# Rows of the last two expert items added by 0/1 products on TensorE, pair rows of the other items loaded during the expert loops

## The chip, the cores and the metric

The kernel is one program on one core of a Trainium2 chip. Its metric is the device time of one execution in microseconds (us), lower is better. Three executions of the kernel before took 1325.0, 1329.38 and 1330.95 us; the median is 1329.38 us.

## The reference, cut to what matters

Two layers of a backbone run over 256 context tokens and 256 latent tokens of 1024 numbers. A layer norms its tokens, projects them, mixes them in three head groups (SSD, long convolution, mLSTM), projects back and adds; then a second norm feeds a mixture of experts, whose output is multiplied by a gate vector and added to the stream. Of this the change touches the last part:

```
grp_prob = softmax(t @ grp_router_w + b);  group = argmax            # 4 groups
top_w, top_idx = top-2 of 8 experts inside that group                # 2 of 32 experts for each token
hid = silu(t @ w_gate[e]) * (t @ w_up[e])                            # 1024 -> 256
out[t] = sum over the token's two experts of top_w * (hid @ w_down[e])   # 256 -> 1024
x = x + mod[5] * out
```

In the first layer 512 tokens are routed (1024 token-expert pairs), in the last one only the 256 latent tokens (512 pairs). After the last layer the latent rows are normed once more and written out.

## The kernel before, in words

**Items.** The experts' work is cut into items: one expert with up to 64 of its tokens (`ITEM_ROWS`). Layer 0 has 33 items (`EXPERTS + EXTRA[0]`), layer 1 has 32. Three weight matrices of 1 MB belong to an item: gate, up, down. For item j GpSimd gathers the token rows from `h2_rows` in DRAM (`rows(j)`), TensorE transposes them (`gathered`), multiplies them by the gate and up matrices (`gate_up`), transposes the hidden rows (`hidden`) and multiplies by the down matrix (`down`). The result, scaled by the routing weight, goes to `res_v[:, j % 2, :]`: by ScalarE in layer 0 (`weighted`), by VectorE, with the gate vector too, in layer 1 (`gated_halves`). Its partitions 0 to 63 hold the first 512 numbers of the 64 rows, partitions 64 to 127 the other 512. GpSimd scatters it to `pair_rows` in DRAM: each token has two rows there, one for each of its experts (`y` = 0, 1).

**Weights.** SyncE (the queue SP) issues all weight loads in one order. Up to 18 places of SBUF (`pieces`) hold an expert matrix; `expert_slots` says which place the n-th matrix takes and behind the use of which earlier matrix (`behind`) it may be loaded. `taken_again` says whether a place is used again.

**The end of a layer.** After the last weight load SP issues the first two loads of the next layer's in-projection (`next(loading[l + 1])`, layer 0 only). Then it waits until the last two scatters have landed and loads `pair_rows`, one 1 MB DMA per token tile t of 128 tokens, in the order 2, 3, 0, 1 (layer 1: 2, 3) into the areas `two_v[l][t]` (L616, L618). All engines but SP and GpSimd meet at `stage_end(l, "moe")`. A block `If(flag != 0)` handles more than 33 (32) items; it isn't entered in the profiled execution.

**The start of layer 1.** VectorE works through the tiles: `pair_sum` (the two rows of a pair added), `pair_gate` (times the gate row), `pair_add` (added to `x`). ScalarE takes the squares of the new `x` for the norm. VectorE turns them into factors (`inverse`), the rows are scaled (`xn`, tile 2 by ScalarE, the others by VectorE), TensorE transposes them (L780) into all eight PSUM banks (`blocks`), ScalarE and VectorE copy them to `hT` (`input_columns`), and then the in-projection begins with the long convolution's columns (`hy`), which need the latent tiles 2 and 3 only. The context tiles 0 and 1 follow: their transposes (L761) stand on TensorE behind the first `hy` chunk and one product for the modulation, and wait for the rows `xn` of tile 1. `busy(b, n)` issues n products of no use, each two passes of 256 columns, while TensorE would else be idle: 11 ahead of the transposes of tile 2, 5 ahead of those of tile 3.

**The end of layer 1.** VectorE: sum 2, add 2, sum 3, `inverse(2)`, add 3, `normed_output(2)`, `inverse(3)`, `normed_output(3)`; then the output DMAs.

A bank of PSUM is taken in turn by `product(name)`, which makes TensorE wait at once until the bank's old content has been read. An fp32 product appears in the profile as two passes (records). L647 is the helper `mm`, L1778 `tt`, L1781 `stt`, L1784 `copy`, L1774 `ts`, L1391 `fn` (ScalarE).

## Time and profile before

| | us |
|---|---|
| executions | 1325.0, 1329.38, 1330.95 |
| the profiled execution: its time | 1326.25 |
| its span in the profile | 1324.4 |
| TensorE matmuls busy | 1169.2 (88%) |
| VectorE, ScalarE, GpSimd busy | 605.8 (46%), 305.8 (23%), 133.2 (10%) |

```profile
PE   6799999999889989999777689998889899998882
DVE  5434996038963641432111266973393533332223
ACT  4202112265352202131111232131442100000001
PEclk8899999999899989999998899998999899998897
DMA  8743233337651679999999745441474879999982
```

Each digit is the busy share in one of 40 equal slices of the span (33 us), in tenths. The stretches with a DMA digit of 9 (about 490 to 745 us and 1070 to 1290 us) are the two expert loops, where the 99 and 96 weight matrices stream in. PEclk is the granted clock of TensorE in tenths of 2.4 GHz. The boundary between the layers lies at 745 to 785 us.

### The profile page before, as it was taken

How to read it: one execution, taken by the hardware profiler on the slowest of the kernel's cores; microseconds unless marked ns; L12 is line 12 of the kernel's file. 1: busy time of each engine (PE TensorE's matmuls, PEld its weight loads, DVE VectorE, ACT ScalarE, POOL GpSimd, SP SyncE). 2: the span in 40 equal slices, each digit the busy share in tenths (PEclk: the TensorE clock that was granted, in tenths of full speed). 3: DMA queues.
4: the chain of work that ended last, by engine and by line, in shares of the span. 5: the costliest groups of instructions: out<-in, count | busy, mean ns of one | idle time of the engine just before them, and what ended most of it. 6: DMA issues, size and time to landing. Idle time of an engine off the chain costs nothing. (4 is left out here: it accounts for less than half of the span.)

```text
span 1324.4 us, 19485 instructions
## 1 busy us (share of the span) xinstructions
PE 1169.2 (88%) x7596; PEld 769.5 (58%) x7596; DVE 605.8 (46%) x1233; ACT 305.8 (23%) x623; POOL 133.2 (10%) x144
## 2 busy tenths in 40 slices
PE   6799999999889989999777689998889899998882
PEld 3444547977679855555444466467768655545551
DVE  5434996038963641432111266973393533332223
ACT  4202112265352202131111232131442100000001
POOL 0000000000000012222121100000000112221220
PEclk8899999999899989999998899998999899998897
DMA  8743233337651679999999745441474879999982
GB/s 288 200 157 110 82 111 96 100 121 233 206 193 38 261 260 382 390 384 371 374 390 376 268 158 166 128 141 48 160 269 187 350 303 391 386 389 395 397 338 111
DMA packets 146421, 321.40 MB, mean 243 GB/s; under 512 B 28217, under 2 KB 111222, under 8 KB 121368
## 3 DMA queue, kind: packets, MB, share of 16 engines
q1 hardware_dynamic: 134840, 304.08, 63.5%
q0 software_dynamic: 11392, 15.79, 3.7%
q8 instruction: 63, 1.03, 0.3%
q14 instruction: 30, 0.25, 0.1%
q10 hardware_dynamic: 96, 0.26, 0.0%
HBM read 320.32 MB, written 21.23 MB: 258 GB/s over the span
## 5 line engine op out<-in xcount | busy, mean ns | idle before, releaser
L647 PE MATMUL bank<-hT,ring 128*128 128x512 f32 (+1 forms) x544 | 207.4, 539 | 1.8 <-DVE hT L1774 1.8
L647 PE MATMUL bank<-ring,hT 128*128 128x256 f32 (+1 forms) x928 | 181.9, 351 | 8.4 <-DVE chain L1784 3.9
L647 PEld LDWEIGHTS bank<-ring,hT 128*128 128x128 f32 x928 | 155.2, 195 | 28.0 <-issue 7.0
L647 PE MATMUL bank<-chain,qkT 128*64 128x256 f32 (+1 forms) x792 | 144.8, 386 | 19.7 <-DMA chain<-in_moe_w_up 5.5
L647 PEld LDWEIGHTS bank<-hT,ring 128*128 128x128 f32 x544 | 104.2, 194 | 98.6 <-issue 91.7
L1778 DVE TENSOR_TENSOR ktok<-ktok,bank 64x256 f32<-64x256 f32 x65 | 27.5, 423 | 281.1 <-ACT ktok L1391 217.4
L1391 ACT ACTIVATE ktok<-bank 64x256 f32<-64x256 f32 (+2 forms) x79 | 32.1, 406 | 350.6 <-PE bank L647 295.6
L647 PEld LDWEIGHTS bank<-chain,qkT 128*64 128x64 f32 (+1 forms) x792 | 86.7, 152 | 40.0 <-issue 20.4
L1324 POOL DMA_INDIRECT pair_rows<-hyT,ysum x65 | 65.7, 1011 | 385.0 <-ACT hyT L1391 197.7
L647 PE MATMUL bank<-ring,qkT 128*64 128x256 f32 x528 | 84.1, 393 | 10.1 <-DMA ring<-in_moe_w_up 5.7
L1391 ACT ACT_TABLE_LOAD x33 | 42.3, 1283 | 111.2 <-PE bank L647 68.0
L1319 POOL DMA_INDIRECT big<-h_rows,ysum x65 | 61.7, 950 | 47.2 <-DVE ysum L1778 28.0
L647 PEld LDWEIGHTS bank<-ring,qkT 128*64 128x64 f32 x528 | 51.8, 141 | 25.1 <-issue 8.3
L647 PE MATMUL bank<-big,qkT 128*64 128x256 f32 x256 | 60.3, 390 | 1.8 <-DMA chain<-in_moe_w_up 1.4
L1333 POOL DMA_DIRECT2D grow<-in_b_mod x4 | 2.3, 584 | 589.0 <-ACT grow L1391 589.0
L1204 PEld LDWEIGHTS bank<-ident,big 64*128 64x128 f32 x520 | 37.6, 140 | 36.6 <-issue 24.8
L647 PE MATMUL bank<-ident 128*128 128x256 f32 x188 | 50.9, 426 | 8.7 <-DMA hT<-pair_rows 7.8
L647 PE MATMUL bank<-hT,qkT 128*64 128x256 f32 x272 | 50.6, 426 | 8.6 <-DMA hT<-in_moe_w_up 6.7
L1784 DVE COPY qkT<-bank 128x512 f32<-128x512 f32 x65 | 45.0, 692 | 24.1 <-PE bank L1204 22.3
L1204 PE MATMUL bank<-ident,big 64*128 64x64 f32 x520 | 46.1, 229 | 9.0 <-DMA big<-h_rows,ysum 5.3
L1227 PEld LDWEIGHTS bank<-ident,ktok 64*128 64x128 f32 x130 | 20.4, 204 | 55.0 <-DVE qkT L1784 37.3
L1778 DVE TENSOR_TENSOR big<-big,bank 128x384 f32<-128x384 f32 x48 | 26.6, 554 | 54.6 <-ACT big L1391 52.1
(298 smaller groups left out, 1718.0 us busy)
## 6 DMA issues: line engine op xcount, KB each, us to landing
ring<-in_w_mod SPq DMA_DIRECT2D x40, 1024.0 KB
chain<-in_moe_w_up SPq DMA_DIRECT2D x23, 1024.0 KB
ring<-in_w_in SPq DMA_DIRECT2D x22, 1024.0 KB
chain<-in_moe_w_down SPq DMA_DIRECT2D x19, 1024.0 KB
chain<-in_moe_w_gate SPq DMA_DIRECT2D x19, 1024.0 KB
ring<-in_moe_w_down SPq DMA_DIRECT2D x18, 1024.0 KB
ring<-in_moe_w_up SPq DMA_DIRECT2D x17, 1024.0 KB
ring<-in_moe_w_gate SPq DMA_DIRECT2D x16, 1024.0 KB
```

Source lines behind the costliest of these rows:

```text
L647: return nc.tensor.matmul(o, a, b, start=s, stop=e, **k)
L1204: last = nc.tensor.transpose(b[:, k * R:(k + 1) * R], rows_v[r0:r0 + R, j % 2, k * P:(k + 1) * P], ident[r0:r0 + R, r0:r0 + R])
L1227: last = nc.tensor.transpose(b[:, f * R:(f + 1) * R], hid_v[0:R, j % 2, f::2], ident[0:R, 0:R])
L1319: return nc.gpsimd.indirect_dma_start(dst, None, h2_rows, bass.IndirectOffsetOnAxis(at_, 0), bounds_check=NT * P - 1, oob_is_err=False)
L1324: return nc.gpsimd.indirect_dma_start(pair_halves, bass.IndirectOffsetOnAxis(at_, 0), src, None, bounds_check=2 * MOST_PAIRS - 1, oob_is_e ...
L1333: pool.dma_start(modrow(m)[2:3, :], A["b_mod"][l:l + 1, m * D:(m + 1) * D]).then_inc(gate_bias_in[l][n], tick(f"gate_bias{l}{n}_in", ("gat ...
L1391: step(nc.scalar.activation(o, i, f, **k), *names)
L1778: step(V.tensor_tensor(o, a, b, op), *names)
L1784: step(V.tensor_copy(o, a), *names)
```

## The change: what it does

- The results of a layer's last two items aren't scattered. From item `items_now - 6` on, VectorE has built 0/1 matrices (`late_rows`, `late_hot`): for each of the two items 64 rows by the 128 tokens of a tile, once for each half of the partitions. TensorE multiplies them with the results (`late`): four products for each tile, into two banks. VectorE adds the two banks to the summed pair rows (`pair_late`, two additions of 512 columns).
- Ahead of item 0's scatter, GpSimd scatters zeros to the rows of the last two items (`zeros scattered`), so that the sum over `pair_rows` is right without them.
- SP no longer waits for the last two scatters ahead of the pair loads, but for those of the two items before them. The areas of tiles 2 and 3 must be free by then: `PAIR_PLACES`, `LAST_IN_PAIRS` keep matrices with n > 82 out of them, so that later matrices take other places. The next layer's two first loads come behind the pair loads of tiles 2 and 3.
- TensorE and VectorE no longer wait for the other engines at the end of the expert stage; they do so inside `If(flag != 0)`.
- At the start of layer 1, VectorE's order becomes: sum 2, sum 3, late 2, gate 2, add 2, small columns, `inverse(2)`, late 3, gate 3, add 3, ... TensorE's becomes: `late` of tiles 2 and 3, small columns, transposes of tiles 2 and 3 with their `busy` products, `late` of tiles 0 and 1, in-projection. At the end of layer 1: sum, late, add of tile 2, then of tile 3, then `inverse(2)`.
- In layer 1 VectorE also clears `big[:, 0:2048]` during the out-projection (the gathered rows of an item beyond its tokens must be numbers now, since they are multiplied by 0).

The diff, cut to its core (left out: declarations, the constant `steps`, the block behind `flag`, where `res_more` takes the place of `res_v[:, 0, :]`):

```diff
+PAIR_PLACES, LAST_IN_PAIRS = ((4, 5), (14, 4)), 82
@@ -122,7 +123,7 @@
-    return l > 0 or s not in (8, 10) or n <= LAST_IN_TAPS
+    return (l > 0 or s not in (8, 10) or n <= LAST_IN_TAPS) and (s not in PAIR_PLACES[l] or n <= LAST_IN_PAIRS)
@@ -337,6 +340,11 @@
+        late_hot = (ktok[:, 0:1024].rearrange("p (n t c) -> p n t c", n=2, t=NT),
+                    ysum[:, 0:512].rearrange("p (n t c) -> p n t c", n=2, t=2))
+        late_token, late_step = ysum[:, 512:514], ysum[:, 514:530].rearrange("p (n b) -> p n b", n=2)
+        res_more = chain[:, 2048:2560]
@@ -494,7 +502,7 @@
                             for const, t in (("gsel", gsel), ("mask", ysum[:, 1024:1024 + 2 * P]), ("keep", keep),
-                                             ("iom", iom), ("inv", inv)):
+                                             ("iom", iom), ("inv", inv), ("steps", steps)):
@@ -594,10 +602,6 @@
-                if l + 1 < DEPTH:
...
-                    for _ in range(2):
-                        next(loading[l + 1])
@@ -612,10 +616,23 @@
-                for n in (1, 2):
+                def last_in(s):
+                    return ("used", ("expert", l, max(n for n in range(matrices) if places[n] == s)))
...
+                sp.wait_ge(*due(("zeros scattered", l)))
+                for n in (4, 3):
                     sp.wait_ge(*due(("scattered", l, EXPERTS + EXTRA[l] - n)))
-                for t, two in two_v[l].items():
-                    sp.dma_start(two, pair_rows.rearrange("(y t p) d -> t p y d", y=2, p=P)[t]).then_inc(
+                for t in two_v[l]:
+                    if t >= 2:
+                        sp.wait_ge(*due(last_in(PAIR_PLACES[l][t - 2])))
+                    elif t == 0:
+                        for _ in range(2):
+                            next(loading[l + 1])
+                        sp.wait_ge(*due(("made", ("gathered", l, EXPERTS + EXTRA[l] - 1))))
+                    else:
+                        sp.wait_ge(*due(last_in(8)))
+                        sp.wait_ge(*due(("made", ("spec", l + 1, 3))))
+                    sp.dma_start(two_v[l][t], pair_rows.rearrange("(y t p) d -> t p y d", y=2, p=P)[t]).then_inc(
@@ -722,6 +739,21 @@
+            def late(l, tiles):
...
+                items_now, t0 = EXPERTS + EXTRA[l], 0 if l == 0 else 2
+                b = {(t, half): product(("late", l, t, half)) for t in tiles for half in range(2)}
+                pe.wait_ge(*due(("late hot", l)))
+                for n in range(2):
+                    j = items_now - 2 + n
+                    pe.wait_ge(*due(("result", l, j)))
+                    for t in tiles:
+                        for half in range(2):
+                            rows = slice(ITEM_ROWS * half, ITEM_ROWS * half + ITEM_ROWS)
+                            last = mm(b[t, half][:, :], late_hot[l][rows, n, t - t0, :], res_v[rows, j % 2, :], n == 0, n == 1)
+                        if n:
+                            last.then_inc(pe_done, made(("late", l, t)))
@@ -769,17 +801,17 @@
                 else:
+                    late(l - 1, (2, 3))
...
                     for t in range(2):
-                        if t == 0:
-                            pe.wait_ge(*due(("pairs", l - 1, 2)))
...
                                 last.then_inc(pe_done, made(("h1", l, k, 1)))
+                    late(l - 1, (0, 1))
@@ -1259,8 +1291,10 @@
                 down(items_now - 1)
-                stage_end(l, "moe")
+                pe.drain().then_inc(pe_done, tick("pe_done", ("end", "pe", l, "moe")))
                 with pe.If(flag != 0):
+                    pe.wait_ge(*due(("end", "act", l, "moe")))
+                    pe.wait_ge(*due(("end", "dve", l, "moe")))
@@ -1292,6 +1326,8 @@
                     pe.wait_ge(more_dve[l], (MORE_ITEMS - EXTRA[l]) * MORE_DVE[l])
+                if l + 1 == DEPTH:
+                    late(l, (2, 3))
@@ -1355,9 +1391,15 @@
                         pool.wait_ge(*due(("pair table", l)))
+                        pool.wait_ge(*due(("zeros", l)))
+                        for late in (2, 1):
+                            scatter(res_v[:, 1, :], pair_of[:, items_now - late:items_now - late + 1]).then_inc(
+                                zeros_out[l], tick(f"zeros{l}_out", ("zeros scattered", l), by=16))
...
                         flag = pool.value_load(more_flag[0:1, :], min_val=0, max_val=MORE_ITEMS)
+                    if j >= items_now - 2:
+                        continue
@@ -1728,6 +1770,8 @@
                         act.wait_ge(*due(("scattered", l, j - 2)))
+                    elif j:
+                        act.wait_ge(*due(("zeros scattered", l)))
@@ -1814,6 +1858,13 @@
+            def pair_late(l, t):
+                two = two_v[l][t]
+                dve.wait_ge(*due(("made", ("late", l, t))))
+                for half in range(2):
+                    cs_ = slice(512 * half, 512 * half + 512)
+                    tt(two[:, 0, cs_], two[:, 0, cs_], bank(("late", l, t, half))[:, :], ADD, ("read", ("late", l, t, half)))
@@ -1894,10 +1945,7 @@
-                if l:
-                    step(V.memset(va_v[:, :, :, HD:HD + 1], 1.0))
-                    small_columns()
-                else:
+                if l == 0:
@@ -1931,12 +1979,16 @@
                     pair_sum(l - 1, 2)
-                    pair_gate(l - 1, 2)
-                    pair_add(l - 1, 2)
                     pair_sum(l - 1, 3)
-                    inverse(l, 2, 1)
-                    pair_gate(l - 1, 3)
-                    pair_add(l - 1, 3)
+                    for t in (2, 3):
+                        pair_late(l - 1, t)
+                        pair_gate(l - 1, t)
+                        pair_add(l - 1, t)
+                        if t == 2:
+                            dve.wait_ge(*due(("end", "pe", l - 1, "moe")))
+                            small_columns()
+                            inverse(l, 2, 1)
+                    step(V.memset(va_v[:, :, :, HD:HD + 1], 1.0))
@@ -1945,9 +1997,11 @@
                         input_columns(k, ("h1T", l, 1, "dve"))
+                    pair_late(l - 1, 0)
...
                     pair_sum(l - 1, 1)
+                    pair_late(l - 1, 1)
@@ -2400,6 +2454,8 @@
                         logits(order[n - 1])
+                    if l and n == 0:
+                        step(V.memset(big[:, 0:2048], 0.0))
@@ -2509,6 +2565,8 @@
                         dve.wait_ge(*due(("scattered", l, j - 2)))
+                    elif j:
+                        dve.wait_ge(*due(("zeros scattered", l)))
@@ -2516,7 +2574,20 @@
+                def late_rows():
...
+                    first_tile = t0 // 2 * 4
+                    copy(late_token, token_of[:, items_now - 2:items_now])
+                    tt(late_step, late_token.unsqueeze(2).broadcast_to([P, 2, 8]),
+                       steps[:, 64:72].unsqueeze(1).broadcast_to([P, 2, 8]), SUB)
+                    blocks = 8 - first_tile
+                    for n in range(2):
+                        tt(late_hot[l][:, n, :, :].rearrange("p t (h c) -> p (t h) c", c=64),
+                           steps[:, 0:64].unsqueeze(1).broadcast_to([P, blocks, 64]),
+                           late_step[:, n, first_tile:].unsqueeze(2).broadcast_to([P, blocks, 64]), ALU.is_equal, ("late hot", l))
...
                 rows_columns(0)
+                step(V.memset(res_v[:, 1, :], 0.0), ("zeros", l))
@@ -2541,10 +2612,14 @@
                         filter_step(l + 1, 5, (j - FILTER_ITEMS[5],))
+                    if j == items_now - 6:
+                        late_rows()
...
                     gated_halves(items_now - 1)
-                stage_end(l, "moe")
+                dve.drain().then_inc(dve_done, tick("dve_done", ("end", "dve", l, "moe")))
                 with dve.If(flag != 0):
+                    dve.wait_ge(*due(("end", "pe", l, "moe")))
+                    dve.wait_ge(*due(("end", "act", l, "moe")))
@@ -2559,22 +2634,24 @@
             pair_sum(DEPTH - 1, 2)
+            pair_late(DEPTH - 1, 2)
...
             pair_sum(DEPTH - 1, 3)
+            pair_late(DEPTH - 1, 3)
+            pair_add(DEPTH - 1, 3)
...
-            pair_add(DEPTH - 1, 3)
@@ -2614,7 +2691,8 @@
     c = dict(ident=np.eye(P), gsel=gsel, mask=mask, keep=keep, dft=dft, inv=inv / L, feats=feats, tcol=tcol,
-             tri=p[:, None] < p[None, :], iota=np.tile(p % ITEM_ROWS, (P, 1)), items=np.tile(np.arange(ITEMS), (P, 1)),
+             tri=p[:, None] < p[None, :], iota=np.tile(p % ITEM_ROWS, (P, 1)),
+             steps=np.tile(np.concatenate([np.arange(64), 64 * np.arange(8)]), (P, 1)), items=np.tile(np.arange(ITEMS), (P, 1)),
```

## Rows read from the trace of the kernel before

**Rows 1.** The chain that ended last, in order of time: start, duration, what.

```profile
1306.89 6.95 DMA hT<-pair_rows
```

**Rows 2.** Timeline, end of layer 1: start, duration, engine, line, operation [idle before <- releaser].

```profile
1294.60 1.00 POOL L1324 DMA_INDIRECT pair_rows<-hyT,ysum  x1 [9.27 <-DVE ysum L1784]
...
1302.05 0.75 DVE L1781 SCALAR_TENSOR_TENSOR hyT<-bank,ysum,grow 128x512 f32<-128x512 f32 x1 [2.22 <-PEq L658]
...
1311.33 1.23 DVE L1778 TENSOR_TENSOR big<-big 128x1024 f32<-128x1024 f32 x1 [8.53 <-DMA big<-pair_rows]
...
1315.20 0.15 DVE L1774 TENSOR_SCALAR small<-small 128x1 f32<-128x1 f32 x1
```

**Rows 3.** Timeline, layer boundary, GpSimd, SP, VectorE and ScalarE.

```profile
737.36 1.00 POOL L1324 DMA_INDIRECT pair_rows<-hyT,ysum  x1 [5.49 <-ACT hyT L1391]
...
747.16 0.97 POOL L1324 DMA_INDIRECT pair_rows<-hyT,ysum  x1 [1.91 <-ACTq L1309]
...
750.11 0.92 SPq L618 DMA_DIRECT2D hT<-pair_rows  x2
...
755.05 1.23 DVE L1778 TENSOR_TENSOR hT<-hT 128x1024 f32<-128x1024 f32 x1 [7.37 <-DMA hT<-pair_rows]
...
758.89 1.06 ACT L1391 ACTIVATE chain<-x 128x1024 f32<-128x1024 f32 x1 [10.67 <-DVE x L1778]
...
766.90 2.28 DVE L1774 TENSOR_SCALAR hT<-bank,ab 128x256 f32<-128x256 f32 x4 [0.65 <-PE bank L780]
...
780.23 0.75 DVE L1775 TENSOR_SCALAR big<-x,small 128x1024 f32<-128x1024 f32 x1 [0.40 <-ACT small L1391]
```

**Rows 4.** Timeline, layer boundary, TensorE.

```profile
743.64 1.94 PE L647 MATMUL bank<-chain,ysum 128*64 128x512 f32 x8 [0.57 <-DVEq L1309]
...
755.10 7.20 PE L647 MATMUL bank<-ident 128*128 128x256 f32 x22 [7.79 <-DMA hT<-pair_rows]
...
763.03 2.32 PE L647 MATMUL bank<-ident 128*128 128x256 f32 x10
766.30 1.16 PE L780 MATMUL bank<-ident,big 128*128 128x128 f32 x8 [0.94 <-DVE big L1775]
769.28 8.83 PE L647 MATMUL bank<-hT,ring 128*128 128x256 f32 x32 [1.82 <-DVE hT L1774]
...
781.13 2.24 PE L761 MATMUL bank<-ident,big 128*128 128x128 f32 x16 [2.01 <-DVE big L1775]
```

**Rows 5.** Windows: stretch, length, busy us of each engine, granted TensorE clock, DMA share, GB/s.

```profile
750.00:755.00 5.00, 0.00 (x0) 0.00 (x0) 0.00 (x0) 0.00 (x0) 0.00 (x0) 0.50 0.77 274
```

**Rows 6.** TensorE, products over 64 rows: two groups of the lines, one timeline row.

```profile
L647 PE MATMUL bank<-ktok,ysum 64*128 64x512 f32 x16 | 7.4, 603 | 0.0
...
957.16 0.55 PE L647 MATMUL bank<-chain 64*128 64x195 f32 x4
```

**Rows 7.** Groups of VectorE's lines, shapes apart: busy us, mean ns | idle before.

```profile
L1778 DVE TENSOR_TENSOR chain<-bank,hyT 128x512 f32<-128x512 f32 x12 | 8.3, 692 | 33.2 <-PE bank L647 22.4 <-ACT hyT L1391 10.6
...
L1902 DVE MEMSET chain<- 128x1560 f32 x1 | 1.4, 1358 | 0.4 <-DVE ysum L1774 0.4
```

**Rows 8.** Timeline, first scatter and VectorE between two items, layer 0.

```profile
492.74 1.01 POOL L1324 DMA_INDIRECT pair_rows<-hyT,ysum  x1 [18.84 <-ACT hyT L1391]
...
495.69 0.42 DVE L1778 TENSOR_TENSOR ktok<-ktok,bank 64x256 f32<-64x256 f32 x1 [3.84 <-PE bank L1204]
```

**Rows 9.** Timeline, last expert load of layer 0, and TensorE's last item.

```profile
707.70 5.45 SPq L543 DMA_DIRECT2D chain<-in_moe_w_down  x1
...
737.30 3.67 PE L647 MATMUL bank<-chain,qkT 128*64 128x256 f32 x32 [1.17 <-DMA chain<-in_moe_w_up]
```

**Rows 10.** Timeline, out-projection of layer 1: VectorE, then TensorE's transposes.

```profile
1014.45 0.16 DVE L1781 SCALAR_TENSOR_TENSOR small<-small 128x1 f32<-128x1 f32 x1 [0.92 <-ACT big L1391]
...
1016.58 1.05 PE L1109 MATMUL bank<-ident,big 128*128 128x128 f32 x8
```

More of the change, by code:

```diff
@@ L195, in build @@
         more_rows_out = [sem(f"more_rows{l}_out") for l in range(DEPTH)]
+        zeros_out = [sem(f"zeros{l}_out") for l in range(DEPTH)]
         more_weights = [sem(f"more_weights{l}_in") for l in range(DEPTH)]
@@ L222, in build @@
         rw = sb("rw", KB * 36)
+        steps = sb("steps", 72)
         rb = sb("rb", 36)
@@ L1381, in _ @@
                         pool.drain()
-                        scatter(res_v[:, 0, :], index[:, 1:2]).then_inc(more_rows_out[l], 16)
+                        scatter(res_more, index[:, 1:2]).then_inc(more_rows_out[l], 16)
                         pool.wait_ge(more_rows_out[l], i * 16 + 16)
@@ L2561, in _ @@
                         dve.wait_ge(more_pe[l], i * MORE_PRODUCTS + 5)
-                        V.tensor_scalar(res_v[:, 0, :], banks[4][:, :], weight_of[:, bass.ds(i + EXPERTS + EXTRA[l], 1)],
+                        V.tensor_scalar(res_more, banks[4][:, :], weight_of[:, bass.ds(i + EXPERTS + EXTRA[l], 1)],
                                         None, MUL).then_inc(more_dve[l], 1)
@@ L2566, in _ @@
                             dve.wait_ge(more_dve[l], i * MORE_DVE[l] + 5)
-                            V.tensor_tensor(res_v[:, 0, :], res_v[:, 0, :], gate_halves, MUL).then_inc(more_dve[l], 1)
+                            V.tensor_tensor(res_more, res_more, gate_halves, MUL).then_inc(more_dve[l], 1)
                     dve.wait_ge(more_dve[l], (MORE_ITEMS - EXTRA[l]) * MORE_DVE[l])
```

## The prediction

> **What bounds the kernel now.** I read the page first: the loops' DMA digits of 9 and TensorE's 88% say that the middle is full of weights and matmuls. Then the chain of waits, which ends in a transfer of pair rows [rows 1] and VectorE's last norm. Then the timelines at both layer ends. At the end of layer 1 the last result is read from its bank at 1302.05 [rows 2], but the first pair sum starts only at 1311.33: 9.3 us less 0.75 of reading go to a scatter, its landing, an issue and a load. At the layer boundary the same hole: the last scatter at 747.16, SP's issue at 750.11, the first sum at 755.05 [rows 3], with TensorE idle 7.79 [rows 4] and its granted clock at 0.50, the lower of its two levels [rows 5]. The change goes for these two holes. Elsewhere it must not lengthen the expert loops.
>
> **Base.** Durations come from the execution of 1326.25 us (span 1324.4), 3.1 below the median 1329.38 of the three runs; the four times scatter over 6 us.
>
> **End of layer 1.** A scatter needs 2.95 from start to SP's next issue (747.16 to 750.11) [rows 3]. That of item 29 starts at 1294.60 [rows 2], so SP issues both pair loads at 1297.6; they land 4.9 (750.11 to 755.05) and 6.95 after issue [rows 1, 3]: 1302.5 and 1304.9. So the products set the pace. TensorE is free at 1301.9; drain and branch, with no row of their own, cost about 0.4 (0 to 1). A stage of `late` for one item is four products as eight passes of 512 columns, in two halves that lie in different halves of the array, as in `down`: 1.94 [rows 4]. Item 30's part: 1302.3 to 1304.2; item 31's for tile 2 another 1.0: 1305.2. VectorE, which sums tile 2 meanwhile: late 2 is two additions from a bank at 0.69 [rows 7] with their gaps, 1.42; add 2 1.26; sum 3 1.26; late 3 1.42; add 3 1.26 (1.23 each plus the gap [rows 2]): 1311.8. There `inverse(2)` starts, which started at 1315.20 [rows 2]. What follows (table load, root, two norms, output) is unchanged. **Gain 3.4.** Bounds: VectorE alone without waits for products would be 0.6 earlier (gain 4.1); products one after the other are a rival below (gain 1).
>
> **Boundary, up to the transposes of tile 3.** Item 30's scatter starts at 737.36 [rows 3]: landed 740.3, pair loads issued, tiles 2 and 3 in at 745.3 and 747.9. Sums 2 and 3 end at 749.2; late 2 is made at about 748.9 (746.0 after `down` [rows 4], 1.94, 1.0). Then VectorE: late 2, gate 2, add 2 (1.42 + 1.26 + 1.26): 753.2, where before `x` of tile 2 was ready at 758.8 (its squares begin at 758.89 [rows 3]). ScalarE squares it (1.06 and 0.2 for the accumulator [rows 3]), `inverse(2)` ends at 754.9, late 3 at 756.3. So far 4 to 6 us are won. But TensorE takes its eight `blocks` behind `late`: eight banks are all there are, so `product` waits until late 3 has been read, 756.3. Only then do the 11 `busy` products start. Before, they began with the landed pairs at 755.10 and took 7.20, from the lower clock [rows 4, 5]; TensorE will have idled since 750, some 6 us, so the same: 763.5, though the rows of tile 2 wait since 757. Transposes 1.1, five `busy` products 2.32 [rows 4]: the transposes of tile 3 start at 766.7 against 766.30 [rows 4], although VectorE has their rows at 762. **Loss 0.4** (with the higher clock the 22 passes take 5.1 by the 2.32 for ten: a gain of 1.7).
>
> **Boundary, tiles 0 and 1.** `late(l - 1, (0, 1))` stands between those transposes and the in-projection. It needs four banks that `input_columns` has read: 1.2 after the columns begin (767.3 instead of 766.90 [rows 3]), so 768.5. Late 0 is made three quarters through two stages of 1.94: 771.4; late 1 at 772.4. The in-projection starts there, not at 769.28 [rows 4]. VectorE, done with its columns at 769.6, waits 1.8 for late 0; then late 0 1.42, gate, add, sum 1 3.78, late 1 1.46, gate, add 2.52: 780.6. Before, five operations ended 6.3 after 769.2, at 775.5. **Loss 5.1**: the two additions 2.9, the wait 1.8, and the 0.4 carried on. The rows of tile 1, scaled at 780.23 + 0.75 [rows 3], come at 786.1. This is on the path: TensorE, in order, already waited 2.01 there, at 781.13 [rows 4]. The `hy` chunk and the modulation product are over by 781 in any case, so TensorE idles some 5 us before 786. It will start again at the lower clock; before, after a like idle, 22 passes took 7.20 instead of 5.1 [rows 4]. **Loss 2.1** (0 to 2.3). Boundary in sum: 5.1 + 2.1 = 7.2, the 0.4 being in the 5.1. Bounds: 2.5 (warm `busy` products, no second fall of the clock) to 9.
>
> **Expert loops.** The zeros' memset (0.45, by 0.87 ns a column [rows 7]) and two scatters of about 1.3 fit before item 0's scatter, ahead of which GpSimd idles 18.84 [rows 8]. `late_rows` is a copy and three small or middle operations, at most 2 us in layer 0, while VectorE idles about 3.8 before each item's product with the gate [rows 8]; its cover gone, it would cost its 2 us once. The two last scatters fall away where they hid nothing. SP: I worked the order of places through from `expert_slots`. In layer 1 the last load stays behind a matrix of item 26. In layer 0 the last (n = 98) moves from behind a matrix of item 28 to one of item 29, some 8 us; SP had issued it at 707.70 against a full queue (5.45 for one issue), and its neighbour was used only at 737.30 [rows 9], so some 25 us of loads lay ahead of it. Cost 0, with the rival below as bound. The two in-projection loads now go out behind the pairs at about 741 and are needed at 772. The constant's load in layer 0 is one more issue of 0.5, beside matmuls: 0 (to 0.5).
>
> **Clearing of `big`.** 2048 columns at 0.87 ns [rows 7] are 1.8 us, 0.92 of them in the wait for the squares [rows 10]; the scaled rows come 0.9 later, at 1016.9, and the transposes stood at 1016.58 [rows 10]. **Loss 0.3** (0 to 0.9).
>
> **Sum.** 7.2 + 0.3 - 3.4 = +4.1. On the profiled execution 1330.4, on the median 1333.5; I take the middle, 1332. The change would move two DMA latencies off the path and put VectorE additions, products and idle `busy` work in their place.
>
> **Two rules of the Trainium skill.** Four passes of 195 columns over two halves of the rows took 0.55, drain included [rows 6]; one after the other they would take 4 x 0.18 (256 columns are 0.23 [rows 4]) = 0.71 and the drain. So halves overlap. The Trainium skill, "TensorE: Matmul & The Clock Gate", Part 3 (Packing small matmuls), gives 3.07 times for four row tiles, not 4: by that efficiency two tiles would give 1.5 instead of 2, an estimate of 0.8 more at late 0 and 0.5 more at the end, sum +5.4. And "TensorEngine Tiling (Array Packing)", Key Properties, says that a change of the tiling mode drains the engine, which speaks against `late` between full-height matmuls; no row prices it apart.
>
> **Rivals.**
> Faster, the boundary gives what the loads promise: the bank wait and `busy` don't hold TensorE, tile 3's rows are transposed when ready (762.1 instead of 766.2) and late 0 hides under the columns, so that only the 2.9 of additions stay: -1.2, and the end gives 3.4 to 4.1; with slack behind the boundary that takes up these 2.9 too, -8. Against it: the order of `product` and `busy` in the code and TensorE's full slices behind 790. Time 1321 to 1324.
> Slower, the halves don't overlap: a pass of 512 columns over 64 rows takes 0.46 where one half only is used [rows 6], so late 0 comes at 768.5 + 12 x 0.46 = 774.0 (+2.6) and the end's late 2 2.7 later. Sum +9.4, time 1337 to 1339. It decides from late 0 later than 773. The row of 0.55 speaks against it.
> Slower, the last loads of layer 0 run dry: with two places fewer, n = 98 lands up to 8 late and `down(32)` waits: +4.1 + up to 8, 1338. Against it the 25 us of queue.
> No pair load early: if tiles 2 and 3 landed as late as before (their area or scatter not free), the end loses its gain: +8. Nothing speaks for it; the areas are last used at matrices 76 and 77.
>
> **Chances.** Forecast case 0.62 (own range 1326 to 1337); faster rival 0.12; halves in series 0.10; loads run dry 0.06; no early load 0.03; the rest 0.07, mostly that in-order waits behind 790 add up. What can be told from no change here is 0.5%, 6.6 us, so 1322.7 to 1336.0. The forecast case lies there but for its upper end. Faster 0.11, same 0.61, slower 0.28. The range 1323 to 1340 takes in both bounds of the boundary and the series rival.
>
> **What would show it.** The first pair sum at about 745.5 and, in layer 1, before 1304; eight passes of `late` in 1.9, not 3.7; 22 `busy` passes starting only behind late 3's second addition, at about 756, in about 7 us; VectorE waiting about 1.8 for late 0; the transposes L761 5 us later against the first pair scatter of item 30 than before, with TensorE idle before them for 4 to 6 and a slow second `hy` chunk behind. At the end `inverse(2)` 3.4 nearer to the last result. It is wrong if the distance from 737.36 to the transposes L761 (43.8) grows by less than 2, or if `down(32)` or layer 1's item 31 waits longer for its matrix than now.

## The result and the profile after

| | before | after |
|---|---|---|
| median of 12 executions each, us | 1329.16 (1325.0 to 1335.58) | 1333.07 (1330.15 to 1335.63) |
| ratio after / before, 95% | | 1.0031 (1.0018 to 1.0045) |
| profiled execution / its span | 1326.25 / 1324.4 | 1335.13 / 1333.3 |

The kernel became slower by 0.3%, less than the 0.5% that counts as a change here; 1332.0 was predicted. The two profiled executions differ by more (8.9 us) than the medians (3.9). 3.9 of the 8.9 are there already before the first gather of layer 0's experts (469.19 us after the start before, 473.10 after); in the profiles of this study that point lay between 468.2 and 469.2 in the kernels without the added constant load (before, e8, e16) and between 469.1 and 474.7 in the others, and e5 and e6, which don't differ ahead of it, lie 5.6 apart. Whether the constant costs something there is not shown. So in what follows I compare medians, and distances within a profile.

Busy time on the page, after (before: 1169.2, 769.5, 605.8, 305.8 and 133.2):

```profile
PE 1189.9 (89%) x7644; PEld 779.7 (58%) x7644; DVE 619.7 (46%) x1256; ACT 305.6 (23%) x623; POOL 133.3 (10%) x144
```

VectorE has 23 instructions and 14 us more, TensorE 48 matmul passes and 21 us more. The 48 passes of `late` are 11.1 of the latter (three times 3.70 in the rows below); part of the rest is matmuls at the lower clock.

Layer boundary of the kernel after, GpSimd, SP and VectorE (start, duration, engine, line, operation, [idle before <- what ended it]); it answers to [rows 3]:

```profile
741.78 0.98 POOL L1360 DMA_INDIRECT pair_rows<-hyT,ysum  x1 [5.50 <-ACT hyT L1433]
...
744.53 0.90 SPq L635 DMA_DIRECT2D hT<-pair_rows  x2
...
749.43 1.22 DVE L1822 TENSOR_TENSOR hT<-hT 128x1024 f32<-128x1024 f32 x1 [2.74 <-DMA hT<-pair_rows]
...
753.34 1.41 DVE L1822 TENSOR_TENSOR hT<-hT,bank 128x512 f32<-128x512 f32 x2
...
759.00 1.41 DVE L1822 TENSOR_TENSOR hT<-hT,bank 128x512 f32<-128x512 f32 x2
...
765.57 0.75 DVE L1819 TENSOR_SCALAR big<-x,small 128x1024 f32<-128x1024 f32 x1 [0.40 <-ACT small L1433]
771.00 2.28 DVE L1818 TENSOR_SCALAR hT<-bank,ab 128x256 f32<-128x256 f32 x4 [4.68 <-PE bank L811]
775.44 1.41 DVE L1822 TENSOR_TENSOR big<-big,bank 128x512 f32<-128x512 f32 x2 [2.16 <-PE bank L664]
...
789.33 0.75 DVE L1819 TENSOR_SCALAR big<-x,small 128x1024 f32<-128x1024 f32 x1 [0.40 <-ACT small L1433]
```

The same stretch of TensorE, which answers to [rows 4]:

```profile
749.67 3.70 PE L664 MATMUL bank<-hyT,ktok 64*128 64x512 f32 x16 [0.90 <-ACTq L1345]
753.31 0.29 PE L786 MATMUL bank<-ident,prow 78*128 78x78 f32 x1
760.66 6.96 PE L664 MATMUL bank<-ident 128*128 128x256 f32 x22 [7.07 <-ACT big L1433]
767.47 1.04 PE L811 MATMUL bank<-ident,big 128*128 128x128 f32 x8
768.35 2.32 PE L664 MATMUL bank<-ident 128*128 128x256 f32 x10
770.51 1.04 PE L811 MATMUL bank<-ident,big 128*128 128x128 f32 x8
772.49 3.70 PE L664 MATMUL bank<-hyT,ktok 64*128 64x512 f32 x16 [0.94 <-DVE hT L1818]
776.12 7.17 PE L664 MATMUL bank<-hT,ring 128*128 128x256 f32 x32
...
790.23 3.65 PE L793 MATMUL bank<-ident,big 128*128 128x128 f32 x16 [5.94 <-DVE big L1819]
793.68 7.92 PE L664 MATMUL bank<-hT,ring 128*128 128x256 f32 x32
```

And windows of it (stretch, length, busy of PE, PEld, DVE, ACT, POOL, granted clock, DMA share, GB/s):

```profile
755.00:760.00 5.00, 0.00 (x0) 0.00 (x0) 3.75 (x7) 2.05 (x4) 0.00 (x0) 0.78 1.07 383
760.00:765.00 5.00, 4.33 (x11) 3.53 (x12) 4.67 (x9) 1.60 (x3) 0.00 (x0) 0.53 1.05 375
...
790.00:795.00 5.00, 4.77 (x20) 4.51 (x21) 1.59 (x4) 3.80 (x7) 0.00 (x0) 0.50 0.26 80
```

The reader is to see three things. The pair loads go out 2.75 us behind the scatter of item 30, and the first sum starts 7.65 behind it (before: 17.69 behind it, since the loads waited for the last scatter). What they win is gone at 770.51: tile 3's rows are scaled at 766.3 (765.57 + 0.75), but TensorE, which stood still from 753.6 to 760.66 until late 3 had left the banks, still works through `busy` passes. Then the context tiles take the longer way: TensorE waits 5.94 for tile 1, and what follows runs at 1.2 GHz (clock 0.50).

End of layer 1 after, with [rows 2] as its counterpart:

```profile
1313.88 0.75 DVE L1825 SCALAR_TENSOR_TENSOR hyT<-bank,ysum,grow 128x512 f32<-128x512 f32 x1 [2.22 <-PEq L1294]
...
1315.34 1.23 DVE L1822 TENSOR_TENSOR big<-big 128x1024 f32<-128x1024 f32 x1 [0.71 <-DVEq L2619]
1317.59 1.41 DVE L1822 TENSOR_TENSOR big<-big,bank 128x512 f32<-128x512 f32 x2 [1.03 <-PE bank L664]
...
1324.25 0.15 DVE L1818 TENSOR_SCALAR small<-small 128x1 f32<-128x1 f32 x1
```

`inverse(2)` starts 10.37 after the last result's reading begins, where it was 13.15: the hole of a scatter, its landing and a load (8.53 idle) is gone. TensorE's row there:

```profile
1314.64 3.70 PE L664 MATMUL bank<-hyT,ysum 64*128 64x512 f32 x16 [0.89 <-DVEq L2619]
```

Distances in the profiles of all kernels (us). **ctx**: from the scatter of layer 0's item 30 to the transposes of tiles 0 and 1. **3rd**: from there to the third `hy` chunk, which stands behind everything that the boundary delays. **gather**: to layer 1's first gather. **end**: from the last result's reading to `inverse(2)`. **last**: from the scatter of item 30 to the product of the last item with its down matrix, which ends the layer's expert work.

| kernel | last | ctx | 3rd | gather | end | median | ratio to before, 95% |
|---|---|---|---|---|---|---|---|
| before | 6.3 | 43.8 | 53.9 | 314.5 | 13.15 | | 1 |
| after | 5.1 | 48.5 | 60.8 | 322.7 | 10.37 | 1333.07 | 1.0031 (1.0018 to 1.0045) |
| e1_end_only | 5.0 | 42.5 | 52.6 | 312.9 | 10.38 | 1326.51 | 0.9972 (0.9951 to 0.9993) |
| e2_boundary_only | 6.5 | 49.9 | 62.6 | 324.7 | 12.99 | 1334.83 | 1.0042 (1.0023 to 1.006) |
| e3_no_busy | 6.6 | 45.5 | 57.3 | 318.9 | 10.43 | 1329.14 | 0.9993 (0.9978 to 1.0008) |
| e4_no_context | 5.2 | 44.3 | 55.9 | 314.0 | 10.43 | 1324.78 | 0.9956 (0.994 to 0.9972) |
| e5_turned | 6.6 | 49.6 | 62.0 | 320.5 | 10.37 | 1329.63 | 0.9999 (0.9985 to 1.0013) |
| e6_ctx_later | 6.6 | 52.5 | 55.7 | 318.4 | 10.44 | 1324.53 | 0.996 (0.9942 to 0.9977) |
| e7_early_late | 6.5 | 43.8 | 53.9 | 311.6 | 10.37 | 1323.13 | 0.9946 (0.993 to 0.9961) |
| e8_before_turned | 6.6 | 44.0 | 55.4 | 313.1 | 12.81 | 1326.19 | 0.9968 (0.9954 to 0.9982) |
| e13_early_ctx | 6.3 | 47.1 | 49.0 | 308.7 | 10.37 | 1318.87 | 0.9913 (0.9892 to 0.9933) |
| e14_early_ctx_clear | 5.1 | 46.4 | 48.3 | 304.8 | 10.42 | 1317.83 | 0.9913 (0.9896 to 0.993) |
| e15_end_both | 6.3 | 47.7 | 49.6 | 308.9 | 10.42 | 1321.10 | 0.9941 (0.9919 to 0.9964) |
| e16_before_both | 6.6 | 50.0 | 51.9 | 314.6 | 13.08 | 1323.17 | 0.9944 (0.9927 to 0.9961) |

Each is compared with executions of the kernel before on the same chip (medians 1329.82 for e1 to e4, 1329.36 for e5 to e8, 1329.75 for e13 to e16). Where a text below takes the medians of two kernels from different chips, those four medians of the kernel before (1329.16 to 1329.82) say how far that can be off, and ratio and quotient of the medians differ by up to 0.0008, 1.1 us. The distances are of one profile each: between e1 and before, whose boundary is the same, `3rd` differs by 1.3.

That difference is `last`: 5.0 in e1, 6.3 before. It is a matter of how the last two items happened to follow one another, and every distance from item 30's scatter has it in it. Counted from the last item's product instead (`ctx` less `last`), the context transposes stand at 37.5 before and in e1, and at 43.4 in after and e2. So the boundary costs 5.9 up to them, not the 4.7 of the table's first two rows, and 8.1 up to the third chunk, not 6.9. A distance can also hold a stretch at the lower clock that has nothing to do with the change; two such follow below (e15, e16). In e6 and e13 to e16 the context transposes stand behind the second chunk, so there only `3rd` compares.

### The profile page after: what moved, and what is told of

Its sections match the earlier page's. It is cut to its first block and busy times, and to the rows that moved or that the text cites. A ratio compares the mean times of both kernels' runs of the same rounds, so it can differ in the third digit from the quotient of the medians.

```text
span 1333.3 us, 19619 instructions
## 1 busy us (share of the span) xinstructions
PE 1189.9 (89%) x7644; PEld 779.7 (58%) x7644; DVE 619.7 (46%) x1256; ACT 305.6 (23%) x623; POOL 133.3 (10%) x144
## 5 line engine op out<-in xcount | busy, mean ns | idle before, releaser
L664 PE MATMUL bank<-chain,qkT 128*64 128x256 f32 (+1 forms) x808 | 151.0, 391 | 11.5 <-DMA hT<-in_moe_w_up 4.0
L664 PEld LDWEIGHTS bank<-chain,qkT 128*64 128x64 f32 (+1 forms) x808 | 90.0, 154 | 32.8 <-issue 7.0
L664 PE MATMUL bank<-ring,qkT 128*64 128x256 f32 x496 | 93.3, 424 | 11.7 <-DMA ring<-in_moe_w_up 5.5
L664 PEld LDWEIGHTS bank<-ring,qkT 128*64 128x64 f32 x496 | 54.9, 153 | 31.1 <-issue 16.0
L664 PE MATMUL bank<-big,qkT 128*64 128x256 f32 x272 | 68.0, 407 | 5.5 <-DMA chain<-in_moe_w_up 4.5
L1236 PEld LDWEIGHTS bank<-ident,big 64*128 64x128 f32 x520 | 37.5, 139 | 36.4 <-issue 26.5
L1822 DVE TENSOR_TENSOR big<-big,bank 128x384 f32<-128x384 f32 (+1 forms) x52 | 29.3, 564 | 59.8 <-ACT big L1433 54.0
L1433 ACT ACTIVATE grow<-bank 128x256 f32<-128x256 f32 (+1 forms) x53 | 21.4, 404 | 128.4 <-PE bank L664 127.9
```

Of the source, the lines that this page charges most:

```text
L664: return nc.tensor.matmul(o, a, b, start=s, stop=e, **k)
L1236: last = nc.tensor.transpose(b[:, k * R:(k + 1) * R], rows_v[r0:r0 + R, j % 2, k * P:(k + 1) * P], ident[r0:r0 + R, r0:r0 + R])
L1433: step(nc.scalar.activation(o, i, f, **k), *names)
L1822: step(V.tensor_tensor(o, a, b, op), *names)
```

## The experiments

**The two halves of the change apart.** A flag for each layer chooses the new way or the old one.

```
LATE = (False, True)     # e1: late rows in layer 1 only, at its end
LATE = (True, False)     # e2: late rows in layer 0 only, at the boundary
```

> The change at the end of layer 1 alone (layer 0 and its boundary as before). My theory: from the last result's read to inverse(2) 10.4 us as in the changed kernel, against 13.2 before; the clearing of big costs TensorE 0.7 at the transposes of the out-projection. Time 2 us below before, ratio 0.998. Rival (the end hides nothing, the time is set by the output): ratio 1.000 or more.

> The change at the layer boundary alone (end of layer 1 as before). My theory: from the scatter of item 30 to the context tiles' transposes 48.4 us against 43.8 before, and a start at the lower clock worth 2 more: time 6.5 to 7 us above before, ratio 1.005. Rival (the boundary is neutral, the expert loops carry the loss): ratio 1.000 to 1.001, and the loops longer by 4.

Measured 1326.51 (3.3 us below before) and 1334.83 (5.0 above). The two add up to +1.7, where the whole change gives +3.9; the intervals, 2.8 and 2.5 us to each side, cover the difference. So the end, with the clearing of `big` that goes with it, gives about 3, and the boundary takes more; the rival that puts the loss into the expert loops is excluded: in e2 they are shorter than before (first gather to item 30's scatter 266.5 for 268.2 in layer 0, first gather to last scatter 248.3 for 251.7 in layer 1). Both signs are shown, and neither half is hidden by slack.

**The `busy` passes behind the banks.**

```
-  busy(blocks[0], (11, 5)[t])
+  busy(blocks[0], (0, 5)[t])
```

> The changed kernel without the 11 busy products ahead of tile 2's transposes (the 5 ahead of tile 3's stay). My theory: tile 2's transposes start when its rows and the banks are there, 7 us earlier; tile 3's behind five busy products at the lower clock (10 passes, 4.3), some 3 us earlier than in the changed kernel; the chain to the context tiles' transposes 3 us shorter, less up to 1.5 for late products at the lower clock. Time 1.5 to 3 us below the changed kernel, ratio to before 1.001 to 1.002. Rival (the busy products pay for themselves by the clock): equal to the changed kernel or slower, ratio 1.003 to 1.005.

Measured 0.9993, 3.9 us better than after (1333.07 to 1329.14). I expected less, since the lower clock should have been paid by the next work. It was paid, but not in full:

```profile
759.47 1.94 PE L811 MATMUL bank<-ident,big 128*128 128x128 f32 x8 [6.47 <-ACT big L1433]
761.21 4.33 PE L664 MATMUL bank<-ident 128*128 128x256 f32 x10
765.38 1.05 PE L811 MATMUL bank<-ident,big 128*128 128x128 f32 x8
```

Tile 2's transposes start as soon as its rows are there and cost 0.90 more at the lower clock (1.94 for 1.04), the ten passes 2.01 more (4.33 for 2.32): 2.9 against the 6.96 that the 22 passes take. The distance `ctx` falls by 2.9, `3rd` by 3.5; counted from the last item's product, by 4.5 and 5.0. So passes that warmed TensorE beside a DMA wait stand on the path once the wait is gone.

**The context tiles without their late rows.** Left out are the products and additions of the last two items' rows for tiles 0 and 1.

```
-                    late(l - 1, (0, 1))
...
-                    pair_late(l - 1, 0)
...
-                    pair_late(l - 1, 1)
```

> The changed kernel without late products and additions for the context tiles 0 and 1 at the boundary (their rows of the last two items are left out of the result). My theory: VectorE saves 2.9 of additions and the 2.2 wait for them, so the context tiles' transposes come 5 us earlier, and TensorE saves its 3.7: time 5 us below the changed kernel and 1 below before, ratio 0.999. Rival (in-order waits behind absorb it): less than 2 us below the changed kernel, ratio 1.002.

Measured 0.9956, more than any of the estimates: 8.3 us below after. By distances 4.9 are won at the third chunk, as the steps say (the additions and the wait for late 0). Another 3.8 are won behind it, where nothing was taken out. The only thing that differs there is which bank each product gets: `product` hands the eight banks out in turn, and without the four banks of `late(0, 1)` every later product stands four banks away. That called for the next pair.

**The turn of the banks, alone.** Nothing but the counter is moved.

```
                     late(l - 1, (0, 1))
+                    turn[0] += 4
```

In e8 the same line stands in the kernel before.

> The changed kernel with the turn of the PSUM banks moved on by four ahead of the in-projection of layer 1, nothing else. The run without context additions came out 3 us better than its boundary explains, and its TensorE wait of 3.9 for a bank of the state products was gone; its turn of banks stood four further. Theory (the turn is the cause): that wait gone or below 1, the stretch from the third hy chunk to the first gather of layer 1 3 us shorter, time 3 us below the changed kernel, ratio to before 1.001. Rival (the missing additions freed VectorE later on): wait unchanged, ratio 1.003.

> The kernel before with the turn of the banks moved on by four ahead of the in-projection of layer 1. Theory (the turn alone is worth 3 us, whatever the boundary does): ratio 0.9975, the wait of 3.9 gone. Rival (the gain belongs to the changed boundary): ratio 1.000.

Measured 0.9999 (after: 1.0031) and 0.9968: by the medians 3.4 and 3.2 us of pure bank numbering, by the ratios 0.32% in both, which is 4.2 us. In the mixers of layer 1, products named `ys` and `st` always take bank 4 and `mn` bank 7; the projections beside them take banks in turn and, in the old numbering, come upon one that VectorE has yet to read. TensorE of the kernel before, then of e8:

```profile
904.23 13.45 PE L647 MATMUL bank<-ring,hT 128*128 128x256 f32 x64 [3.88 <-DVE chain L1784]
```

```profile
900.34 10.75 PE L647 MATMUL bank<-ring,hT 128*128 128x256 f32 x64
...
914.42 0.66 PE L885 MATMUL bank<-ident,chain 128*128 128x128 f32 x4 [1.60 <-DVE chain L1785]
```

And the clock of either behind it, windows of the kernel before, then of e8:

```profile
904.50:909.50 5.00, 5.00 (x13) 3.92 (x13) 0.00 (x0) 0.00 (x0) 0.00 (x0) 0.50 0.00 0
```

```profile
904.50:909.50 5.00, 5.00 (x33) 4.59 (x32) 0.00 (x0) 0.49 (x1) 0.00 (x0) 1.00 0.02 3
```

A wait of 3.88 goes and one of 1.60 comes; and the 64 passes, which ran in part at 1.2 GHz behind the longer wait, take 2.70 less. 3.88 + 2.70 - 1.60 = 5.0, of which 2.9 and 3.5 arrive at the gather (`3rd` to `gather`: 260.6 before, 257.7 in e8; 262.0 after, 258.5 in e5).

**The context transposes later.** The latent half of the third chunk needs nothing of tiles 0 and 1, and the second chunk neither.

```
                 for q in range(3):
                     channel_major("hy", 6, q, lambda blk: n0)
-                    if l and q == 0:
+                    if l and q == 1:
```

(the same on ScalarE, which copies them.)

> The changed kernel with the context tiles' transposes (and their copies on ScalarE) moved behind the second hy chunk. Theory (TensorE stands at these transposes and then starts at the lower clock): the wait of 5.9 gone or below 1, the second chunk 7.1 instead of 7.9 and the transposes 2.2 instead of 3.7, time 7 to 8 us below the changed kernel, ratio to before 0.997. Rival (VectorE's chain is the bound behind as well, so the wait only moves): less than 3 us below the changed kernel, ratio above 1.001.

Measured 0.996, 8.5 us below after. TensorE's rows:

```profile
784.70 7.17 PE L664 MATMUL bank<-hT,ring 128*128 128x256 f32 x32
...
792.81 1.61 PE L793 MATMUL bank<-ident,big 128*128 128x128 f32 x12
795.47 0.71 PE L793 MATMUL bank<-ident,big 128*128 128x128 f32 x4 [1.05 <-DVE hyT L1825]
```

The wait of 5.94 and the lower clock behind it are gone: 5.1 at the third chunk. This shows that VectorE's part of the late context rows, the additions and the wait for late 0, cost only because TensorE, in order, had its next work behind them. TensorE's own part stays: `late` of tiles 0 and 1 still stands ahead of the in-projection, which starts 29.6 behind the last item's product (after: 29.3, before: 25.6). e6 differs from after by nothing else, and the 8.5 in the medians is more than the 5.1; the interval of e6 (some 2.3 us to each side) leaves it open whether more was won than that.

**Late products ahead of the transposes.** The small columns go first (on VectorE too), both stages of `late` directly behind, the latent transposes are packed into four banks (tile columns of k and k + 2 in one), and `busy` is cut to 2 and 8 products of 128 columns:

```
-                    late(l - 1, (2, 3))
                     small_columns()
-                    blocks = [product(("h1", l, k, 1)) for k in range(KB)]
+                    late(l - 1, (2, 3))
+                    late(l - 1, (0, 1))
+                    four_banks = [product(("h1", l, k, 1)) for k in (2, 3, 6, 7)]
```

> The changed kernel with the late products of tiles 0 and 1 directly behind those of tiles 2 and 3, the latent transposes packed into four banks instead of eight so that they need only the banks of late 2 and 3, and 2 and 8 short busy products instead of 11 and 5; the turn of banks then stands four further than in the changed kernel. Theory (the eight banks and the place of late 0 and 1 cost the early loads their worth): tile 3's transposes start when its rows are there, 4 us earlier than in the changed kernel; VectorE doesn't wait for late 0; context transposes 42 to 43 behind the scatter of item 30 (48.4 changed, 43.8 before); with the turn's 3 us the time is 9 to 10 below the changed kernel, ratio to before 0.996. Rival (VectorE's own work is the bound): context transposes no earlier than 46, ratio above 0.999.

Measured 0.9946. The 32 passes of `late` run in one piece (748.52, 7.14) beside the loads; tile 3's transposes start at 764.52, 25.5 behind the scatter of item 30 (after: 28.7), and `ctx` is 43.8, as before the change. This version takes four banks fewer, so its turn is the good one too (257.7 from `3rd` to `gather`): of its 9.9 us below after, some 6.9 are the boundary's. The in-projection starts 23.4 behind the last item's product (before: 25.6).

**Together.** e13 is e7 with the context transposes later; e14 in addition clears `big` ahead of the first out-projection sum:

```
+                if l:
+                    dve.wait_ge(*due(("made", ("out", l, MIX_ORDER[l][0], 0))))
+                    step(V.memset(big[:, 0:2048], 0.0))
```

e15 and e16 ask what of it is the change's at all: e15 is e1 (end only) and e16 the kernel before, both with `turn[0] += 4` and the context transposes later. (The labels e9 to e12 have no measurement; they were the same four kernels.)

> The kernel of the early late products (packed transposes) with the context tiles' transposes moved behind the second hy chunk. Theory: its wait of 3.1 for them goes, nothing takes its place: third hy chunk 3 us earlier than 53.9 behind the scatter of item 30, ratio to before 0.992. Rival (VectorE's chain of additions and convolution steps is now the bound): no more than 1 us, ratio 0.994 to 0.995.

> The same, and big is cleared ahead of the first out-projection sum of layer 1 instead of behind it. Theory (the clearing delays the first norm): TensorE's wait of 0.7 at those transposes goes back to below 0.1, 0.7 us less than the run beside it. Rival: VectorE is late for the first sum instead, no change in time.

> The change at the end of layer 1 alone, with the turn of the banks moved on by four and the context transposes behind the second hy chunk; the boundary's pair rows as in the kernel before. Theory (three independent terms: end 2.8 less 0.7 for the clearing, turn 3, context wait 2.0): 7 us below before, ratio 0.9945. Compared with the run of early late products and later transposes it says what early pair loads at the boundary are worth once nothing hides them: 2 to 3 us.

> The kernel before with the turn of the banks moved on by four and the context transposes behind the second hy chunk, no late products. Theory: turn 3 and context wait 2.0, 5 us below before, ratio 0.996. Rival (the two terms hide one another): ratio 0.9975.

Measured 0.9913, 0.9913, 0.9941 and 0.9944. e14's median, 1317.83, is the lowest: 11.9 below before, 15.2 below after. TensorE of e13 shows the boundary without the hole:

```profile
762.10 1.19 PE L664 MATMUL bank<-ident 128*128 128x128 f32 x4 [3.04 <-DVE hT L1827]
...
771.88 8.83 PE L664 MATMUL bank<-hT,ring 128*128 128x256 f32 x32 [2.81 <-DVE big L1827]
...
789.75 2.06 PE L793 MATMUL bank<-ident,big 128*128 128x128 f32 x16
791.65 7.07 PE L664 MATMUL bank<-hT,ring 128*128 128x256 f32 x32
```

The clearing is 1.0 by medians, and the intervals don't separate e13 from e14. e16 says that more than half of the gain needs nothing of the change: three lines in the kernel before give 0.56%. Its `gather`, 314.6 for 314.5 before, seems to say the opposite. But that one profile has some 9 us at the lower clock in which TensorE was busy throughout:

```profile
951.50:956.50 5.00, 5.00 (x34) 4.26 (x34) 2.44 (x5) 0.14 (x1) 0.00 (x0) 0.50 0.36 116
956.50:961.50 5.00, 5.00 (x50) 2.20 (x46) 4.25 (x10) 1.01 (x3) 0.28 (x1) 0.58 0.27 79
```

In e8 the same work, behind the same waits, ran at 1.00, and the stretch between two of TensorE's waits around it took 26.8 there and in the kernel before, 31.6 in e16. So 4.8 of e16's `gather` are this fall, and the twelve executions decide.

e15 and e16 differ by the end and its clearing; the end's 2.7 are in the distances (10.42 for 13.08) and 2.1 in the medians; the ratios (0.9941, 0.9944) don't resolve it. What the early loads at the boundary are worth is e13 against e15: 0.5 by `3rd`, 2.2 by the medians, with intervals that overlap. The 0.5 is too little: in e15's profile the first `hy` chunk ran at the higher clock, in e13's (8.83, above) and e16's partly at the lower:

```profile
773.37 7.14 PE L671 MATMUL bank<-hT,ring 128*128 128x256 f32 x32 [1.83 <-DVE hT L1834]
```

With this 1.7 it is 2.2, and against e16, whose first chunk took 8.83 too, `3rd` is 2.8 shorter in e13. So the distances and the medians agree on 2 to 3 us; the ratios, with overlapping intervals, don't settle it.

## Why the prediction was right

It held by its steps: each wait that it named is there, in its order. The sizes fit less well than this table looks, as the item on the sum says.

| step, as distance | predicted | measured |
|---|---|---|
| item 30's scatter to the first pair sum | 8.1 | 7.65 |
| to the start of the 22 `busy` passes | 18.9 | 18.88 |
| the 22 passes | 7.2 | 6.96 |
| to tile 3's transposes | 29.3 | 28.73 |
| VectorE's wait for late 0 | 1.8 | 2.16 |
| to the context transposes, against before | +5.1 | +4.7 |
| lower clock behind them | 2.1 | 2.3 |
| boundary up to the third chunk | 7.2 | 6.9 |
| end of layer 1 | -3.4 | -2.8 |
| clearing of `big` | 0.3 | 0.7 |

- **Boundary, tile 3.** The bank wait decided it: TensorE idles 7.07 and starts 0.25 behind late 3's last addition (760.41); the profile names ScalarE's scaling, which ended at 760.45 (759.30 + 1.15), but TensorE waits for that one only behind the `busy` products. Since the banks came free just when tile 2's rows were ready, the wait for banks by itself cost nothing; it cost because `busy` began only behind it. The first sum comes 10.0 us earlier, of which 4.3 reach tile 3's rows (scaled 24.5 behind the scatter, 28.9 before); the others go to the late rows' additions and the new order. These 4.3 are lost too, and the transposes of tile 3 stand where they stood (28.73 for 28.94). e3 and e7 confirm that the order of `product` and `busy` kept them from coming through: in e3 tile 3 is transposed 0.4 behind its rows.
- **Boundary, tiles 0 and 1.** +4.7 for +5.1, by luck of `last` as near as that (+5.9 from the last item's product); the 0.4 that tile 3 should have lost was a gain of 0.2. e4 takes 4.9 out at the third chunk. The lower clock: the 16 transposes took 3.65 for 2.24, the chunk behind them 7.92 for 7.07, together 2.3.
- **Halves of the array.** 16 passes of 512 columns took 3.70 in after, at both places: 0.46 for each pair that lies in two halves. In series they would take 7.4 by [rows 6]. That rival is excluded; the two halves overlap in full, where the Trainium skill, "TensorE: Matmul & The Clock Gate", Part 3 (Packing small matmuls), has 3.07 of 4 for four row tiles: the 1.5 estimated from it for two tiles doesn't hold here, and the sum +4.1 stood closer than +5.4.
- **End.** 2.8 for 3.4. I let item 30's part start ahead of item 31's result, 0.4 behind TensorE's last product. The row at 1314.64 shows 0.89 from the last product to the first `late` pass: 16 passes in one piece, 0.76 after the reading of the last result began. Late 2 is so ready 3.71 after that reading began, 0.6 later than forecast, and the 0.6 goes through to `inverse(2)`. The drain and the branch, put at 0.4 without a row, are the term that was too small: e7 and e13, where the small columns follow them in layer 0, show 0.69. The other 0.2 no run separates (the passes start 0.01 behind the reading of item 31's result, and item 30's part needs none of it). e1 has the same 10.38.

```profile
751.53 0.26 PE L786 MATMUL bank<-ident,prow 78*128 78x78 f32 x1 [0.69 <-issue]
```
- **Expert loops.** Nothing, as predicted: layer 0 268.7 from the first gather to item 30's scatter for 268.2, layer 1 241.9 for 242.8. SP's last load of layer 0 goes out 22.6 ahead of item 30's scatter, where it was 29.7 [rows 9]: 7.0 later, 8 had been predicted. The product that uses it (`xtok`) starts 27.7 later and waits for VectorE, not for the load, so that rival is excluded:

```profile
719.14 0.33 SPq L551 DMA_DIRECT2D xtok<-in_moe_w_down  x1
```

```profile
746.84 1.94 PE L664 MATMUL bank<-xtok,ysum 128*64 128x512 f32 x8 [0.57 <-DVEq L2619]
```

The zeros' scatters fit into GpSimd's idle time:

```profile
481.38 1.40 POOL L1360 DMA_INDIRECT pair_rows<-hyT,ysum  x1 [3.58 <-DVE ysum L1822]
...
497.00 0.97 POOL L1360 DMA_INDIRECT pair_rows<-hyT,ysum  x1 [12.91 <-ACT hyT L1433]
```

- **Clearing of `big`.** Its 1.76 started 0.49 behind the last sum, and TensorE waited 0.74 for the tile (before: no wait):

```profile
1025.70 1.76 DVE L2458 MEMSET big<- 128x2048 f32 x1 [0.49 <-DVE x L1822]
...
1029.15 1.13 PE L1141 MATMUL bank<-ident,big 128*128 128x128 f32 x8 [0.74 <-DVE big L1819]
```

In e14, with the clearing earlier, there is none:

```profile
1011.07 1.04 PE L1145 MATMUL bank<-ident,big 128*128 128x128 f32 x8
```

- **Sum.** 6.9 + 0.7 - 2.8 = +4.8 by distances; another +0.6 lies between third chunk and gather and has no cause that I could find. With the boundary counted from the last item's product it is 8.1 + 0.7 - 2.8 = +6.0. The medians say +3.9 (2.4 to 6.0 by the ratio's interval). Counted so, boundary (7.2), clearing (0.3) and end (3.4) were all put too favourably, and what makes the whole less than its parts is open. That 1332 came within 1.1 of the median is in part luck: it was chosen between 1330.4 and 1333.5, and the measured distances would have given 1334 to 1336.

The faster rival named the right condition: the bank wait and `busy` must not hold TensorE. e7, which meets it, is at 1323.13, within the rival's 1321 to 1324, but that is luck: some 3 us of it are the turn of the banks, of which the rival knew nothing.

## What to carry to other kernels

A sum that came ten us earlier brought its rows 4 us earlier, and even that gave nothing while the engine that uses them had queued a fixed piece of work behind a wait for banks: look at what stands in order between the data and its use, and take filler work for the clock out together with the wait that it filled. Work added for rows that are needed later belongs behind work that doesn't need them, here one more projection chunk. Before two profiles are compared by distances, look whether a distance repeats between kernels that don't differ there: here the choice of the starting point moved it by 1.3 us, and a fall of the clock by 4.8. And where some products take banks in turn and others fixed ones, the number at which the turn stands is a parameter worth trying.

## What I had not expected of the hardware

- Bank numbering alone is worth 3.2 to 3.4 us of 1330 by medians, 0.32% by ratios (e5, e8). A wait of 3.88 costs TensorE 2.70 more behind it, because the granted clock is 0.50 in the next 5 us; with no wait it stays at 1.00.
- 22 passes of 256 columns that began at the lower clock took 6.46 (e1) to 7.97 (e6) in ten kernels, 6.96 in after, and 10 at the higher one 2.32. Work that has to be done at the lower clock can as well be useful: eight transposes took 1.94 for 1.04, less than the filler in front of them.
- The clock can fall while TensorE is busy all the time: 0.50 for some 9 us in e16's profile, 1.00 over the same work in e8's.
- Products over 64 rows in two halves of the array overlap in full over 16 passes (3.70).
- From the last product to the first pass behind a drain and a branch TensorE stood 0.89 to 0.90 us in after (both layers), against 0.69 in e13 (layer 0), where the small columns came first.
